# An encoder step on one core: first head's values and gate as one seven-product block, two token sums on GpSimd, some low parts, copies and stores in another order

## What is computed

```
z = x @ w_in[l]          # queries, keys, values of four head groups, forget gates, a SiLU gate of width 2048
logf = log_sigmoid(ff + b_f);  c = cumsum(logf)
mk, mv = split(mem @ w_mem_kv[l])
outs = (fox(fq, fk, fv, logf), band(bq, bk, bv), swa(rope(sq), rope(sk), sv), cross(mq, mk, mv))
y = (concat(outs) * silu(gate)) @ w_out[l]
x = layer_norm(ALPHA * x + y)
```

## Time and profile before

| what | value |
|---|---|
| median of 3 runs | 1881.79 us (1881.53 to 1882.03) |
| the profiled execution's own time | 1881.31 us |
| its span | 1879.5 us |
| busy PE | 1841.1 us (98%) |
| busy DVE | 1480.4 us (79%) |
| busy ACT | 970.0 us (52%) |
| busy POOL | 172.1 us (9%) |
| granted TensorE clock | 0.996 of 2.4 GHz, mean |

### The profile page before, as it was taken

One profiled execution on the slowest core, in us unless ns is written; L12 is line 12 of the kernel. 1 busy time (PEld: TensorE's weight loads), 2 busy tenths in 40 slices (PEclk: granted clock), 3 DMA queues, 4 the chain that ended last, 5 costly groups with the idle time before them and its releaser, 6 DMA issues.

```text
span 1879.5 us, 36206 instructions
## 1 busy us (share of the span) xinstructions
PE 1841.1 (98%) x14704; PEld 1817.9 (97%) x14704; DVE 1480.4 (79%) x2082; ACT 970.0 (52%) x1580; POOL 172.1 (9%) x293
## 2 busy tenths in 40 slices
PE   6999999999999999999999999999999999999996
PEld 6999999999999999999999999999999999999996
DVE  6978877777798896777887688777788888767776
ACT  6455455445545456544573555555554555554444
POOL 0011100000000101000001111000000010100001
PEclk9999999999999999999999999999999999999998
DMA  8623333333333335655664233333233233545563
GB/s 300 235 82 124 123 125 126 116 126 105 114 104 108 111 124 185 225 205 205 221 222 157 78 123 117 119 115 105 103 110 105 96 121 107 191 148 201 197 219 132
DMA packets 71648, 273.84 MB, mean 146 GB/s; under 512 B 10136, under 2 KB 20000, under 8 KB 59184
## 3 DMA queue, kind: packets, MB, share of 16 engines
q1 hardware_dynamic: 44144, 202.12, 31.3%
q0 software_dynamic: 16928, 55.44, 8.6%
q10 hardware_dynamic: 10432, 14.29, 2.1%
HBM read 238.94 MB, written 35.50 MB: 146 GB/s over the span
## 4 chain that ended last, share of the span: by engine, by line
PE 89%; DVE 4%; ACT 4%; issue 2%; DMA 1%; SPq 0%; ACTq 0%; DVEq 0%
PE GB L733 46%; PE GB L645 19%; PE GB L587 8%; PE GB L960 3%; PE AB L674 3%; PE AB L716 3%; PE AB L685 2%; PE GB L602 1%; DMA WR<-in_wt 1%; ACT WH L1104 1%; DVE WL L1700 0%; PE AB L721 0%; ACT S L1034 0%; PE AB L914 0%; PE AB L701 0%
## 5 line engine op out<-in xcount | busy, mean ns | idle before, releaser
L1104 ACT CAST WH<-WR 128x1024 fp32r<-128x1024 f32 x322 | 335.8, 1047 | 405.0 <-PE GB L733 164.8
L1700 DVE TENSOR_TENSOR WL<-WR,WH 128x1024 fp32r<-128x1024 f32 x322 | 393.6, 1228 | 115.5 <-ACT WH L1104 111.5
L733 PE MATMUL GB<-XH,WH 128*128 128x272 f32 x1472 | 426.3, 290 | 2.5 <-DVE WL L1700 2.5
L733 PE MATMUL GB<-TLOW,WH 128*128 128x272 f32 x1472 | 423.8, 288 | 0.0
L733 PE MATMUL GB<-XH,WL 128*128 128x272 f32 x1472 | 423.4, 288 | 0.0
L733 PE MATMUL GB<-XL,WH 128*128 128x272 f32 x1472 | 421.1, 290 | 0.0
L733 PEld LDWEIGHTS GB<-XH,WH 128*128 128x128 f32 x1472 | 277.4, 188 | 3.3 <-DVE WL L1700 2.9
L1020 ACT CAST WH<-WR 128x2048 fp32r<-128x2048 f32 x92 | 175.5, 1908 | 198.0 <-PE GB L645 154.7
L733 PEld LDWEIGHTS GB<-XH,WL 128*128 128x128 f32 x1472 | 277.6, 189 | 0.0
L733 PEld LDWEIGHTS GB<-TLOW,WH 128*128 128x128 f32 x1472 | 276.8, 188 | 0.0
L733 PEld LDWEIGHTS GB<-XL,WH 128*128 128x128 f32 x1472 | 274.2, 188 | 0.4
(11 more groups left out here) (286 smaller groups left out, 2911.5 us busy)
## 6 DMA issues: line engine op xcount, KB each, us to landing
WR<-in_wt SPq DMA_DIRECT2D x92, 1024.0 KB, 4.8
WR<-in_wt SPq DMA_DIRECT2D x184, 512.0 KB, 4.2
XR<-out POOLq DMA_DIRECT2D x64, 136.0 KB, 2.7
out<-OY ACTq DMA_DIRECT2D x24, 272.0 KB, 2.2
o_rest<-BD POOLq DMA_DIRECT2D x20, 272.0 KB, 5.2
out<-OY ACTq DMA_DIRECT2D x8, 544.0 KB, 5.3
out<-KT POOLq DMA_DIRECT2D x16, 272.0 KB, 2.4
out<-VT POOLq DMA_DIRECT2D x16, 272.0 KB, 2.4
```

Source lines behind the costliest of these rows:

```text
L733: mm = pe.matmul(out, w[:, k, :], x[:, k, :], start=(k == 0 and i == 0), stop=(k == KS - 1 and i == 2))
L1104: act.copy(weight_block(p, name)[0], weight_source(name)).then_inc(b_hi, 1)
L1700: dve.tensor_tensor(lo_part, weight_source(name), hi_part.bitcast(F32), ALU.subtract).then_inc(b_lo, 1)
```

## The change

- `PLAIN_TILES` = 2: only K and Q of the first head are plain tiles. V and gate are a block of seven products with scores after p7 and the transposes after p4, as the other heads have them. A layer has 24 blocks, and the slots come out even, so that the last block's a22 needs no slot of its own. The first weight halves of the last head's plain tile now wait for p5, not p2.
- t1 and t4 are made by GpSimd, ahead of its DMAs of logf and `nc_rows`, not by DVE.
- `first_head` of DVE and ACT is written anew for the block; after it, a12, s1 and s4 of the next block are prepared as in other heads.
- In pair heads s1's low part is ahead of `rope_query`; in the last head the copies of probabilities are ahead of `w_lo`.
- `LAST_POOL` = 3, and the stores are issued in the order 0, 1, 2, 5, 3, 6, 4, 7.

The diff, cut to its core:

```diff
-FIRST_TILES = MEM_TILES + HEAD_TILES
+FIRST_TILES = MEM_TILES + PLAIN_TILES
-HEAD_PAIRS = 2 * (2 * GH - 1)
+HEAD_PAIRS = 2 * (2 * GH - 1) + 1
-LAST_POOL = 2
+LAST_POOL = 3
+LAST_STORES = [0, 1, 2, 5, 3, 6, 4, 7]
...
 @ tensor: first_head
-                for j in range(3):
+                for j in range(PLAIN_TILES):
                     gemm(n, m, j)
-                pe.wait_ge(k_low, kl + 1)
-                pe.wait_ge(zf[1], m + 1)
-                scores(FOX, u, fl=l + 1)
-                gemm(n, m, 3)
-                turn_probs(FOX, u)
-                pe.wait_ge(zf[0], m + 2)
-                turn_v()
...
+                two_tiles(l, b, {"p7": all_scores, "p4": all_probs})
...
 @ vector: first_head (its new body)
+                weight_sum(b, "s3")
+                block_lo(b, "a11")
+                block_lo(b, "s3")
+                weight_sum(b, "s2")
+                x_sum_low(l, "t2")
+                k_lo(kl, TOK, FOX.cached)
                 q_lo(1, l * Q_SPLITS)
+                block_lo(b, "s2")
+                block_lo(b, "a12")
+                weight_sum(b, "s1")
+                weight_sum(b, "s4")
+                block_lo(b, "s1")
+                x_sum_low(l, "t1")
+                soft_in(FOX, u, l, 0, places=range(2))
+                block_lo(b, "s4")
+                soft_in(FOX, u, l, 0, places=range(2, NT))
+                take_product(b, "u2")
+                take_product(b, "u3", GA)
+                block_lo(b, "a22")
+                x_sum_low(l, "t4")
...
+                take_product(b, "c11", VT)
+                invert_sums(u)
+                weight_sum(b + 1, "s3")
...
 @ vector: late_head, last blocks
+                block_lo(b, "s1")
                 rope_query(GA, r + 1, u)
-                block_lo(b, "s1")
...
+                    take_probs(SWA, u + 1)
                     w_lo(l * LT + C0, 0)
-                    take_probs(SWA, u + 1)
...
 @ scalar: last_head
-                act.wait_ge(b_pe, ran(d, "p2"))
+                act.wait_ge(b_pe, ran(d, "p5"))
                 w_hi(n, 0, m)
...
 @ gpsimd, after the memory values' stores
+                pool.wait_ge(x_sums, token_sum(l, "t2"))
+                pool.tensor_tensor(t1, t1, t2, ALU.subtract).then_inc(x_sums, 1)
+                pool.tensor_tensor(t4, t4, t2, ALU.subtract).then_inc(x_sums, 1)
```

More of the change, by code:

```diff
@@ L447, in slot @@
         def slot(p, name):
[L449 to L452, removed]
+            return (len(BLOCKS) * (p % SW_PAIRS) + BLOCKS.index(name)) % SLOTS
         def weight_block(p, name):
@@ L531, in load_pair @@
             def load_pair(l, i):
[L533 removed]
+                p, row = l * SW_PAIRS + i, l * WT + H_ROWS + 2 * (i + 1)
                 def load(s, rows, done):
@@ L563, in _ @@
                     load_weights(0, KC // 2, l * LT + O0 + h * KC, l * WT + O_ROWS)
-            for g in range(NG):
+            for g in LAST_STORES:
                 cs = slice(g * GC, (g + 1) * GC)
@@ L1094, in block_hi @@
                 if i == 0 and at < SLOTS:
-                    act.wait_ge(zd, l * LT + MEM_TILES + (4 if at < 2 else 5))
-                elif i == SW_PAIRS - 1 and name == "a22":
-                    act.wait_ge(b_pe, ran(p, "p5"))
+                    act.wait_ge(zd, l * LT + MEM_TILES + (2 if at < 2 else 3))
                 else:
@@ L1133, in first_head @@
                 act.mul(split2(QH), z2(1), SCALE).then_inc(qh, 1)
-                w_hi(n + 3, 1, m + 1)
+                block_hi(b, "s2")
+                block_hi(b, "a12")
+                x_sum_hi(l, "t1")
                 for s in range(2):
@@ L1137, in first_head @@
                     act.wait_ge(o_mv[s], 16 * ((GH // 2) * (l + 1) + 1))
[L1138 to L1143, removed]
-                scale_probs(FOX, u)
[L1145 to L1150, removed]
+                copy_product(b)
+                block_hi(b, "s1")
+                block_hi(b, "s4")
+                exps(FOX, u, range(2))
+                block_hi(b, "a22")
+                x_sum_hi(l, "t4")
+                exps(FOX, u, range(2, NT))
+                block_hi(b + 1, "a11")
+                scale_probs(FOX, u)
+                block_hi(b + 1, "s3")
+                block_hi(b + 1, "s2")
             def take_head(i, u, l):
@@ L1171, in after_head @@
                 take_v(vu)
[L1172 to L1176, removed]
+                block_hi(a, "a12")
+                act.wait_ge(c_out, taken(a - 1, "c21"))
                 gate_tanh(u)
@@ L2362, in _ @@
                     pool.dma_start(ko[l, h], KT[:, :]).then_inc(o_k, 16)
-                    if i:
-                        pool.wait_ge(c_out, taken(b, "c12"))
-                    else:
-                        pool.wait_ge(zf[0], l * (LT // 2) + MEM_TILES // 2 + 3)
+                    pool.wait_ge(c_out, taken(b, "c12"))
                     pool.dma_start(vo[l, h], VT[:, :]).then_inc(o_v, 16)
```

81 lines of the change are left out of this document (37 added, 44 removed).

## The result

The changed kernel takes 1885.01 us (median of 21 runs, 1884.32 to 1888.16), the kernel before 1881.47 beside it on the same chip (21 runs, 1879.63 to 1883.34). The ratio is 1.0022, 95% interval 1.0017 to 1.0028: slower by 3.5 us. The forecast was 1887.6 with a range of 1877.5 to 1892, and 62% on slower by over 0.2%. The direction and the range held; the loss was put too high, and the interval lies on both sides of 0.2%, so that it is slower is shown, that it is slower by more than 0.2% is not. The two profiled executions took 1886.15 and 1881.31 us, 4.8 apart, and their spans differ by 4.9: the profiled one of the changed kernel is 1.1 above its median, and a trace shows one execution only.

The account below looks back on a forecast made before the run. TensorE was taken as the bound (busy 98% of the span), but VectorE, held by GpSimd's sums, in the new first blocks. +8.5 + 3.7 - 5.3 - 0.6 = +6.3 on 1881.31 gave 1887.6 us, range 1877.5 to 1892.

Parts of the forecast that it names:

- The sums on GpSimd: Start of each layer's first head: t1 and t4 take 4.75 us each and hold VectorE, 7.7 us late after the gate scans.
- small gate operations slip past: Rival: 4-partition gate operations are not held beside GpSimd's sums, only 128-partition ones; 1878.4 us, chance 0.13.
- Before p7: First heads: VectorE needs 8.6 us up to q_lo; p7 starts 6.6 us late in layer 0, 2.3 in layer 1.
- Inside the block: First heads from p7 on: VectorE's 25.2 us bound the block; TensorE waits another 4.95 us in layer 0, 4.35 in layer 1.
- the mix: Mix after the first head: its wait for V, 0.6 us in each layer, goes, -1.2 us in all.
- the idle time forecast before p3 or p4: First heads: TensorE waits 4.95 and 4.35 us (layers 0 and 1) before p3, p4 and the transposes of values.
- Layer 1: Layer 1's first head: -3.0 + 2.3 + 4.35 = +3.7 us, next block at 1055.1 where it was 1051.4.
- The waits that go: Mix after the first head -1.2, pair heads -2.5, last head's mix -1.6 us; together -5.3 us.
- The end: Last norm and stores: ten ScalarE chunks save 1.2 us, a third GpSimd subtraction holds VectorE 1.25; -0.6 us taken.
- The first rival: GpSimd's sums cost VectorE nothing, p7 is on time, the change ends faster: 1873.3 us, chance 0.15.

Follow-up runs that it names:

- a_tiny: The changed kernel with both GpSimd sums (t1, t4) cut to 32 columns of one chunk, the rest left out: 1871.95 us, ratio 0.9953.
- a_qfirst: The changed kernel with k's and q's low parts ahead of t2's low part on VectorE: 1887.17 us, ratio 1.0038.
- b_moves: The kernel before with only the two moves (s1's low part ahead of the rotary steps, copies of probabilities ahead of w_lo): 1875.2 us, ratio 0.9969.
- b_end: The kernel before with only the end changed (LAST_POOL = 3 and the new order of stores): 1880.41 us, ratio 0.9997.
- b_poolsums: The kernel before with only t1 and t4 moved to GpSimd: 1883.56 us, ratio 1.0012.
- a_dvesums: The changed kernel with t1 and t4 on VectorE, between s2's weight sum and t2's low part: 1879.31 us, ratio 0.9990.
- a_c12: The changed kernel with c12 taken right behind the next block's a11 low part, ahead of s3's low part and s2's weight sum: 1881.61 us, ratio 1.0008.
- a_latesums: The changed kernel with GpSimd's two sums issued behind the loads of nc_rows, KTC, BI and VC: 1890.3 us, ratio 1.0052.
- a_pieces: The changed kernel with each of GpSimd's two sums cut into eight instructions of one chunk: 1892.79 us, ratio 1.0064.

## Why the prediction was right, and where it was off

- **The sums on GpSimd.** 4.75 us was taken for each; the first ran 4.92 us. "VectorE reaches the end of the forget-gate scans 7.7 us late: 107.6": the first weight sum starts at 107.80, 7.90 behind the 99.90 of before. This is the step that carries the result, and a_tiny shows its worth: 8.4 us in layer 0 and 6.2 in layer 1 (4.06 + 2.11, with 1.5 of the clock in it, below). The rival that small gate operations slip past is dead (3.99 and 5.30 us for 4 partitions).
- **Before p7.** The sum of 8.6 us was 9.9, mainly because the mask add held `k_lo` here, for 1.07 us; the prediction had it behind `q_lo`. p7 started at 117.82, not 116.2.
- **Inside the block.** From p7 to the next block 27.45 us were forecast; it took 25.5 (117.82 to 143.36), 1.6 of the difference being the mask add's hold, which was over by then. The two errors nearly cancel: first head of layer 0 +7.40, forecast +8.5 less 0.6 for the mix. The working counted p7's delay and the bound within the block as two terms, though they are one run of VectorE's, from 107.80 to c12; a_qfirst shows that p7's start has no price of its own. That the sum came out near is in part luck. Of the idle time forecast before p3 or p4 only 1.1 us came, in layer 1 (before p4).
- **Layer 1.** +4.06 against +3.7 less 0.6. The 1.0 missing lies within the clock's fall behind the transposes of V, 1.5 us in this execution; it need not be in the median one. Of the 21 runs the eleven up to the median have mean granted clocks of 0.992 to 0.995, ten of them 0.993 or more, the ten above it 0.991 to 0.993. The prediction looked for a fall of the clock only in layer 0 and only ahead of p3. There it did fall, and cost at most 0.5 us, because VectorE was the bound (36.99 against 36.53 us).
- **The waits that go**: the term that was mis-sized most. Pair and last heads were to bring 2.5 + 1.6 = 4.1; they brought 3.0 + 3.6 = 6.6 here and 6.3 in b_moves. The listed waits understate the time by what the modelled end of a matmul covers, and leave out the short steps that b_moves also took away.
- **The end.** -0.6 was taken; 0.0 was measured here and 0.2 gained in b_end. Here ScalarE's chunks gained 1.3 (1.2 forecast) and the last issue 0.33 (0.6 forecast), and the time from the last issue to the end of the span grew by 0.33.
- Sum by the trace: 7.4 + 4.06 - 6.6 + 0.0 = +4.9, where the forecast had +6.3. By the medians it is +3.5. The difference is that of the profiled executions from their medians (+1.1 and -0.2); it stands in other runs too, 1.5 us in b_poolsums and 1.8 in a_dvesums, so sums of the table are good to 1 or 2 us of a median only.
- **The first rival** (sums that cost VectorE nothing) was worked out as 1873.3; a_tiny, which makes it true by force, gave 1871.95.

## What to carry to other kernels

An operation moved from VectorE to GpSimd is paid for by VectorE where its neighbours read SBUF twice: here 4.8 us of work saved took 7.9. Count most of GpSimd's own duration (here 10.2) as VectorE's cost, and look at what GpSimd's own queue then issues late. An idle time of TensorE inside a stretch that VectorE bounds is no gain to be had (a_qfirst), and the same idle time at the stretch's end counts in full, and more where the clock falls behind it, as it did in the profiled execution (a_c12). Small moves that fill an idle time of the waiting engine brought some 6 us (b_moves), twice what the first heads gain in a_tiny, where the sums are left out (3.1), and here they are better taken alone.

## What the runs showed of the hardware that was not expected

- The turn between the two engines is not always given behind one GpSimd instruction. L2226 got in between the two sums; L1684 of a_latesums, which had started 0.64 us before them, was held through three, 12.57 us, and 12.63 in layer 1. What decides it is open.
- The hold goes both ways. A GpSimd piece of 0.75 us took 3.59 while VectorE's 2.41 us ran (a_pieces), a mask addition 1.22 where 0.24 is on record (a_latesums). Cut into sixteen, the sums went from 10.2 to 20.95 us, while VectorE reached the first weight sum 2.7 us late instead of 7.9.
- TensorE's granted clock was at 1.2 GHz behind idle times of 3.4, 2.8 and 1.7 us (rows above). In layer 1 of the changed kernel a wait of 2.7 us for `q_lo` was followed by full clock, in a_c12 the same wait by fifteen matmuls 0.227 us apart; the wait of 1.7 us for c12 was followed by the fall there and by full clock in a_tiny. The same idle time does not always bring the fall.
- Two VectorE operations that read PSUM (L2224 and L2225, 4x544) kept their 0.72 and 0.77 us under a GpSimd sum of 4.92.
